# A hybrid decoder layer in fp32r on one core: delta-rule rows turned by VectorE and stored by token, early cache loads, a new first load order and regrouped gate products

## The reference

```
proj = x @ w_in          # A q/k/v | B q/k/v | B z | beta | a | gates
A: dilated attention, 3 groups x 4 heads x 64; samples attend to cached keys and values
B: gated DeltaNet, 4 heads of 128: causal conv (4 taps) + SiLU on q/k/v,
   k, q divided by their norm; beta = sigmoid, decay = exp(-exp(A_log) softplus(a + dt))
   kk = (k beta) k^T ; L = strict_lower(kk * decay) + I ; u = solve(L, v beta - ...)
   attn = (q k^T) * decay ; S = S g + k_dec^T u ; o = q_dec S + attn u
   o = rmsnorm(o) * w * silu(z)
merged = gate_a * (o_att @ w_att_out) + gate_b * (o_dn @ w_dn_out)
h = LN1(alpha x + merged @ w_o)
y = LN2(alpha h + (gelu(conv3(h W_a) + b) * (h W_g)) @ w_down)
```

## Time and profile before

| what | value |
|---|---|
| median of 3 runs | 1831.82 us (1828.69 to 1833.61) |
| the profiled execution | 1833.33 us, span 1831.5 us |
| TensorE (PE) busy | 1772.1 us, 97% of the span |
| VectorE (DVE) busy | 862.7 us, 47% |
| ScalarE (ACT) busy | 539.8 us, 29% |
| GpSimd (POOL) busy | 367.3 us, 20% |
| mean granted TensorE clock | 0.987 |
| moved by DMA | 169.17 MB, mean 92 GB/s |

### The profile page before, as it was taken

The page is one execution under the profiler, slowest core; times in us unless marked ns, Lnnn a source line. Parts: engine busy times, 40 slices in busy tenths (PEclk is TensorE's granted clock), DMA queues, the critical chain, the costliest instruction groups (busy, mean ns, idle before and its releaser), DMA issues.

```text
span 1831.5 us, 36738 instructions
## 1 busy us (share of the span) xinstructions
PE 1772.1 (97%) x14932; PEld 1716.6 (94%) x14932; DVE 862.7 (47%) x1573; ACT 539.8 (29%) x1086; POOL 367.3 (20%) x176
## 2 busy tenths in 40 slices
PE   7999999999988999999999999999999999999997
PEld 6999999999977888888999999999999999999996
DVE  2003347675264667765574674441144441144447
ACT  3124334444412333331222342221022221022224
POOL 1121111121111101011132342222222222222230
PEclk9999999999989999999999999999999999999998
DMA  4110112242442323224462113334332111111112
GB/s 175 46 46 30 44 55 79 81 171 98 138 149 86 112 75 112 76 69 169 143 230 81 70 52 122 123 125 145 122 121 97 46 46 47 46 47 46 38 45 93
DMA packets 70015, 169.17 MB, mean 92 GB/s; under 512 B 9440, under 2 KB 41344, under 8 KB 68608
## 3 DMA queue, kind: packets, MB, share of 16 engines
q1 hardware_dynamic: 69184, 166.63, 26.7%
q10 hardware_dynamic: 720, 0.93, 0.1%
HBM read 137.15 MB, written 57.79 MB: 106 GB/s over the span
## 4 chain that ended last, share of the span: by engine, by line
PE 88%; DVE 6%; DMA 2%; issue 2%; ACT 1%; POOL 1%; SPq 0%; DVEq 0%; ACTq 0%; POOLq 0%
PE U L764 57%; PE U L868 8%; PE U L1201 4%; PE U L1296 3%; PE B L764 2%; PE B L854 1%; PE B L829 1%; PE B L846 1%; PE B L1031 1%; PE B L1063 1%; DVE acc L2134 1%; ACT acc L1569 1%; PE B L1159 1%; DVE og L1825 1%; DVE X L1972 0%
## 5 line engine op out<-in xcount | busy, mean ns | idle before, releaser
L675 POOL TENSOR_TENSOR wl<-stage,wh 128x1024 fp32r<-128x1024 f32 x121 | 296.0, 2446 | 1051.9 <-ACT wh L1313 1049.2
L764 PE MATMUL U<-xh,wh 128*128 128x344 f32 x1176 | 383.1, 326 | 0.2 <-ACT qkv L1317 0.2
L764 PE MATMUL U<-xl,wh 128*128 128x344 f32 x1176 | 376.3, 320 | 0.0
L764 PE MATMUL U<-xh,wl 128*128 128x344 f32 x1176 | 376.2, 320 | 0.0
L764 PE MATMUL U<-hh,wh 128*128 128x344 f32 x1048 | 335.9, 321 | 0.3 <-POOL wl L675 0.3
L764 PE MATMUL U<-hh,wl 128*128 128x344 f32 x1048 | 334.5, 319 | 0.0
L764 PE MATMUL U<-hl,wh 128*128 128x344 f32 x1048 | 334.3, 319 | 0.0
L764 PEld LDWEIGHTS U<-xh,wh 128*128 128x128 f32 x1176 | 221.7, 188 | 0.7 <-ACT qkv L1317 0.5
L764 PEld LDWEIGHTS U<-xh,wl 128*128 128x128 f32 x1176 | 221.7, 189 | 0.0
L764 PEld LDWEIGHTS U<-xl,wh 128*128 128x128 f32 x1176 | 221.6, 188 | 0.0
L764 PEld LDWEIGHTS U<-hh,wh 128*128 128x128 f32 x1048 | 197.2, 188 | 0.8 <-issue 0.8
(11 more groups left out here) (381 smaller groups left out, 2754.5 us busy)
## 6 DMA issues: line engine op xcount, KB each, us to landing
stage<-in_wu SPq DMA_DIRECT2D x126, 512.0 KB, 3.6
out_shift<-in_cache SPq DMA_DIRECT2D x16, 1022.0 KB
gate_scr<-gth SPq DMA_DIRECT2D x16, 516.0 KB, 3.0
gates<-gate_scr SPq DMA_DIRECT2D x8, 1032.0 KB, 5.0
dn_scr<-thb SPq DMA_DIRECT2D x12, 512.0 KB, 2.6
qkv<-in_xT SPq DMA_DIRECT2D x4, 1032.0 KB, 10.5
out_y<-acc SPq DMA_DIRECT2D x12, 344.0 KB, 2.4
kvc<-in_cache SPq DMA_DIRECT2D x4, 1024.0 KB, 9.1
```

The costliest lines, as they stand in the source:

```text
L675: nc.gpsimd.tensor_tensor(wl[:, par, :], stage[:, par, :], wh[:, par, :].bitcast(F32), ALU.subtract).then_inc(w_lo, 1)
L764: ins = nc.tensor.matmul(dst, a[:, par, w], col, start=first and n == 0 and m == 0, stop=last and n == len(ks) - 1 and m == 2)
```

## The change

1. **Turn beside attention.** After `silu` of a q, k or v row block, VectorE turns `thb` in blocks of 32x32 into the `pre` buffer of the block before. SP stores it in four pieces to a new array `tok_scr` (12 row blocks, 1024 tokens by 128 features). ScalarE waits for these stores before it refills that buffer.
2. **Delta tiles.** `kq_turned` and `v_turned` load keys, queries and values by token. The twelve transposes of a tile go. ScalarE makes the squares from SBUF (`squares`), and also `kd` and `vp` (`key_sides`, `value_sides`), at levels 2 and 4. VectorE's key norms of the next tile stand at the end of a tile. The turned output goes to another bank (B7 in place of B34), and `late_masks` comes ahead of the first addition.
3. **Sample group.** The cached keys are loaded in blocks 20 and 21 into the part of `qkv` that is free then, the values at the start of the stage. The decay coefficients (`cf`, `gT`) and the first tile's decays are made inside this stage, not behind it.
4. **Gate quarters.** New counts: `S_FILLS` and `FILLS`.
5. **Start.** The first weights are loaded ahead of x, x in pieces of 1, 1, 2 and 4 tiles; the high products of the first unit come ahead of those of `wbr`.

The diff, cut to its core (memory places, declarations and the parts of the sample group that only rename its tiles are left out):

```diff
+        S_FILLS = (5, 3, 21, 27, 4)
...
-        FILLS = {1: (0, 2, 4, 1, (1, 1, 2, 1, 1, 2), 2), 2: (2, 4, 6, 2, (2, 1, 2, 1, 1, 3), 4)}
+        FILLS = {1: (0, 0, 4, 1, (2, 0, 2, 0, 0, 2), 2), 2: (0, 0, 8, 2, (2, 1, 2, 1, 1, 3), 4)}
...
-            for i in range(4):
-                sp.dma_start(xraw[:, 2 * i:2 * i + 2, :], I["xT"][:, 2 * i:2 * i + 2, :]).then_inc(x_in[i], 16)
-                if i == 0:
-                    sp.dma_start(stage[:, 0, :], I["wu"][0]).then_inc(w_in[0], 16)
+            sp.dma_start(stage[:, 0, :], I["wu"][0]).then_inc(w_in[0], 16)
+            for i, (a, b) in enumerate(X_PIECES):
+                sp.dma_start(xraw[:, a:b, :], I["xT"][:, a:b, :]).then_inc(x_in[i], 16)
...
+            def turned_out(f, par):
+
+                sp.wait_ge(rows_turned, f + 1)
+                for q in range(4):
+                    dst = tok_scr[bass.ds(f, 1)].squeeze(0).rearrange("(n t) (q e) -> q t n e", t=QB, e=QB)[q]
+                    sp.dma_start(dst, pre[QUARTER[q], par, 3:3 + SEQ].rearrange("t (n e) -> t n e", e=QB)).then_inc(
+                        turned_stored[par], 16)
...
+            def cached(n, dst, sems):
+
+                g, t = ((0, 0), (0, 1), (2, 0), (1, 0), (1, 1))[n]
+                a = dst is vals
+                src = I[f"cache{g}"].rearrange("b (c j d) e -> (b c) j d e", c=16, d=DIL[g][1])
+                sp.dma_start(dst[:, n], src[:, 4 * t:4 * t + 4, 0, 256 * a:256 * a + 256]).then_inc(sems, 16)
...
+                if isinstance(b, int) and b in (2 * BLOCKS + 4, 2 * BLOCKS + 5):
+                    sp.wait_ge(kv_stored, 48)
+                    for m in ((0, 1) if b == 2 * BLOCKS + 4 else (2, 3, 4)):
+                        cached(m, keys, samp_in)
...
+                    if kind == "dn" or first_z:
+                        turned_out(b - (BLOCKS + 1), 1 - par)
...
-            for x in range(EARLY - 1):
-                load(U_GATE + 3 + x, (x + 1) % 2)
-                gate_out(U_GATE + x, x % 2)
-            sp.wait_ge(samp_pe, 6)
-            sp.dma_start(dcst[:], I["dcst"]).then_inc(dcst_in, 16)
...
+            def kq_turned(t):
+                sp.dma_start(qkt[:], tok_scr[0:8, t * P:(t + 1) * P, :].rearrange("f t e -> t f e")).then_inc(kq_in, 16)
+
+            def v_turned(t):
+                sp.dma_start(dv[:], tok_scr[8:12, t * P:(t + 1) * P, :].rearrange("f t e -> t f e")).then_inc(v_in, 16)
...
+            load(U_GATE + 2, 0)
+            for n in range(SK // 4):
+                cached(n, vals, values_in)
+            kq_turned(0)
             qk_rows(0)
-            v_rows(0)
-            gate_out(U_GATE + EARLY - 1, (EARLY - 1) % 2)
+            v_turned(0)
             sp.wait_ge(g_turned, 1)
             sp.dma_start(g_scr.rearrange("t (h q) -> (t h) q", h=DN_H), gT[:]).then_inc(g_stored, 16)
             sp.wait_ge(g_stored, 16)
             decays(0)
+            for x in range(EARLY - 1):
+                load(U_GATE + 3 + x, (x + 1) % 2)
+                gate_out(U_GATE + x, x % 2)
+            gate_out(U_GATE + EARLY - 1, (EARLY - 1) % 2)
             for i, u, units in tiles():
                 load(u + 2, u % 2)
...
-                    sp.wait_ge(front_done, i * 4 + 2)
-                    v_rows(i + 1)
                     sp.wait_ge(decay_weighted, i + 1)
                     decays(i + 1)
                     after(sp, ks_done, i)
                     qk_rows(i + 1)
+                    sp.wait_ge(kd_ready, i + 1)
+                    kq_turned(i + 1)
                 for x in range(1, units):
                     gate_out(u + x - 1, (u + x - 1) % 2)
                     load(u + x + 2, (u + x) % 2)
+                if i + 1 < TILES:
+                    sp.wait_ge(vp_ready, i + 1)
+                    v_turned(i + 1)
                 gate_out(u + units - 1, (u + units - 1) % 2)
             sp.wait_ge(s_ready, TILES + 1)
...
-            pe.wait_ge(wba_split, 2)
             for k in range(KT):
                 w = slice(k * P, (k + 1) * P)
                 first, last = k == 0, k == KT - 1
                 pe.wait_ge(x_hi, k + 1)
                 for j in range(THIRDS):
+                    nc.tensor.matmul(U[:, j, 0:TW], wh[:, 0, w], xh[:, k, third(j)], start=first, stop=False)
+                if first:
+                    pe.wait_ge(wba_split, 2)
+                for j in range(THIRDS):
                     nc.tensor.matmul(ba_bank[j], wbr[:, k, :], xh[:, k, third(j)], start=first, stop=False)
-                for j in range(THIRDS):
-                    nc.tensor.matmul(U[:, j, 0:TW], wh[:, 0, w], xh[:, k, third(j)], start=first, stop=False)
...
-            beside.run(30)
+            beside.run(S_FILLS[1])
+            pe.wait_ge(dcst_in, 16)
+            gall = babuf[:, 1, 0:TILES, :]
+            tri = dcst[:, D_TRI:D_TRI + P]
+            nc.tensor.matmul(B7[:, 0:32], tri, gall, start=True, stop=True)
+            nc.tensor.matmul(B7[:, 32:64], dcst[:, D_ONE:D_ONE + P], gall, start=True, stop=True)
+            nc.tensor.matmul(B56[0:DN_H * TILES, 0, 0:P], gall.rearrange("p t h -> p (t h)"), tri, start=True,
+                             stop=True).then_inc(cf_pe, 1)
+            beside.run(S_FILLS[2])
+            pe.wait_ge(g_turned, 1)
             pe.wait_ge(samp_dve, 1)
...
-                    ins = nc.tensor.transpose(B34[:, 1, c], of[:, h, :], ident)
+                    ins = nc.tensor.transpose(B7[:, c], of[:, h, :], ident)
...
-                if i < TILES:
-                    pe.wait_ge(dn_in, 32 * i + 32)
-                    after(pe, xt_ready, i * (LEVELS + 1))
-                    for h, c in heads:
-                        ins = nc.tensor.transpose(B7[:, c], dqk[:, i % 2, 4 + h, :], ident)
-                    ins.then_inc(front_done, 1)
-                    beside.run(f_turn)
+                after(pe, xt_ready, i * (LEVELS + 1))
...
-                for h, c in heads:
-                    ins = nc.tensor.transpose(B56[:, 1, c], dv[:, h, :], ident)
-                ins.then_inc(front_done, 1)
-                for h, c in heads:
-                    ins = nc.tensor.transpose(B56[:, 0, c], dqk[:, i % 2, h, :], ident)
-                ins.then_inc(front_done, 1)
                 beside.run(f_keys)
-                after(pe, of_ready, i - 1)
+                pe.wait_ge(dn_in, 16 * i + 16)
+                after(pe, o_ready, i - 1)
                 pe.wait_ge(ao_low, i + 1)
...
+                        if kind == "dn" or isinstance(b, int) and b < 2 * BLOCKS + 6:
+                            after(act, turned_stored[par], (b - (BLOCKS + par)) * 32)
...
+            def squares(t):
+                act.wait_ge(kq_in, 16 * t + 16)
+                nc.scalar.activation(sqk[:], qkt[:, 4:8, :], ACT.Square, scale=0.5).then_inc(squared, 1)
+                nc.scalar.activation(qkt[:, 0:4, :], qkt[:, 0:4, :], ACT.Square, scale=0.5).then_inc(squared, 1)
...
+            def key_sides(t):
+                act.wait_ge(decay_weighted, t + 1)
+                for h in range(DN_H):
+                    ins = nc.scalar.activation(kd[:, t % 2, h, :], qkt[:, 4 + h, :], ACT.Identity, bias=0.0,
+                                               scale=rn[:, 11, h:h + 1])
+                ins.then_inc(kd_ready, 1)
+
+            def value_sides(t):
+                act.wait_ge(k_rooted, t + 1)
+                act.wait_ge(v_in, 16 * t + 16)
+                for h in range(DN_H):
+                    ins = nc.scalar.activation(vp[:, t % 2, h, :], dv[:, h, :], ACT.Identity, bias=0.0,
+                                               scale=rn[:, 2, h:h + 1])
+                ins.then_inc(vp_ready, 1)
...
+                    if lv == 2:
+                        key_sides(i)
                     if lv == 3 and i + 1 < TILES:
                         decay_of(i + 1)
+                    if lv == 4:
+                        value_sides(i)
...
+                if i + 1 < TILES:
+                    squares(i + 1)
...
+                    if kind == "dn" or first_z:
+                        dve.wait_ge(conv_out, b - (BLOCKS - 1))
+                        nc.vector.transpose(pre[:, 1 - par, 3:3 + SEQ], thb[:, 0:SEQ]).then_inc(rows_turned, 1)
...
+                if n == 0:
+                    dve.wait_ge(cf_act, 1)
+                    st.link(nc.vector.tensor_copy(cf[:, 0, 0:32], B7[:, 0:32]))
+                    nc.vector.tensor_tensor(cf[:, 3, 0:32], B7[:, 32:64], cf[:, 0, 0:32], ALU.subtract).then_inc(cf_dve, 1)
+                    nc.vector.tensor_scalar(cf[:, 4, 0:32], cf[:, 0, 0:32], -1.0, None, ALU.mult).then_inc(cf_dve, 1)
...
+            def decay_rows(t):
+                dve.wait_ge(g_in, 16 * t + 16)
+                nc.vector.tensor_tensor(ET[:], ET[:], same(dcst[:, D_NEG:D_NEG + P]), ALU.add).then_inc(decay_sum, 1)
+
+            decay_rows(0)
...
+                if t > 1:
+                    out_gated(t - 2)
...
-                dve.wait_ge(k_rooted, t + 1)
-                dve.wait_ge(front_done, t * 4 + 2)
```

(10 more changed lines are left out.)

201 lines of the change are left out of this document (87 added, 114 removed).

## The result

| | before | changed |
|---|---|---|
| median of 4 runs | 1832.27 us | 1816.26 us (1815.48 to 1817.69) |
| ratio, 95% interval | 1 | 0.9912 (0.9893 to 0.9932) |
| the profiled execution | 1833.33, span 1831.5 | 1815.48, span 1813.6 |

The account below looks back on a forecast made before the run. TensorE, busy 97% of the span, was taken as the bound. Gains of 2.4 + 7.0 + 7.3 + 9.8 + 4.6 = 31.1 us, from a median of 1831.8, gave 1801 us, range 1788 to 1816.

Parts of the forecast that it names:

- the weighted values end in time: Sample group: with 27 quarters TensorE's wait of 4.5 us for VectorE's weighted values falls to 1.6, and the clock stays.
- the decay row costs 0.4 us: Sample group: VectorE may wait for a decay row queued on SP behind values and rows; 0.4 us set against the gain.
- the first rival: Delta tiles: with the fills gone, levels wait on Y copies and X additions, 1.5 us a tile: 1813, chance 0.13.
- Start, forecast 2.4: Before TensorE's first product: loads ahead of the weights' copy fall from 1544 to 512 KB, gaining 2.4 us.
- Blocks, forecast 0: Twelve attention blocks: VectorE's turn of 1.32 us fits its wait, stores of 3.8 us a block hide behind it; cost 0.
- Sample group, forecast 7.0: Earlier cache loads, moved quarters, a shorter wait for the values and the full clock behind it gain 7.0 us.
- my rival: Sample group: slower strided reductions or a decay row 4 us late keep the wait and lower clock: 1808, chance 0.12.
- First tile, forecast 7.3: The mask wait of 4.7 us goes, with 1.3 of half clock and 1.3 for the twelve transposes.
- the third rival: TensorE's issue pauses of 3.7 us and the slow products round them vanish: 1795, chance 0.08.
- Tiles 1 to 7, forecast 14.4: Fewer transposes and less switching win 1.4 us a tile, 9.8 in all; the wait at the turned output another 4.6.
- I leave the issue pauses in: First tile's forecast: TensorE's issue pauses of 3.7 us are kept in the forecast time.
- The signs: Observations listed beforehand as showing the forecast right, such as first product near 7.4 and tiles 28 us apart.

Follow-up runs that it names:

- x_again: The changed kernel itself, unedited, run once more on the chip of the last group: 1815.37 us, ratio to before 0.9900.
- x_kv_early: Changed kernel, but SP stores keys and values of two of the three groups eight blocks earlier: 1809.90 us, ratio to before 0.9877.
- x_long_runs: Changed kernel, but turned rows are stored as they lie, in 4 KB runs, so the order by token is lost: 1815.57 us in one run.
- x_decay: Changed kernel, but VectorE adds the mask to the first tile's decay rows behind the sample's weighted values; it also waits for all five value loads: 1813.54 us, 0.9878.
- x_sample: Changed kernel with the edits of x_mask and x_decay, the sample's own value product ahead of the cached ones and 34 quarters instead of 27: 1804.09 us, 0.9832.
- x_mask: Changed kernel, but in each tile ScalarE copies the next unit's weights before the gated output, not after it: 1805.84 us, ratio to before 0.9857.
- x_loads2: x_mask, but SP makes all three loads of the next tile at the end of a tile: 1816.38 us, ratio to before 0.9908.
- x_all_loads: x_sample with the early store of x_kv_early, zero products before the first, and the load by features at a tile's end: 1800.05 us, 0.9817.

## Why the prediction was wrong, step by step

The steps that failed are two: in the sample group, that the weighted values end in time and the decay row costs 0.4 us, and in the tiles, that VectorE's product for the mask keeps its length when the order changes. The levels were not left bare, as the first rival had it: TensorE's waits there for the addition to X are 3.1 us in 16 places, and were 4.5 in 23. That the median lies so near the range's end, and that of x_again (1815.37) inside it, is luck: no case of the prediction had this mechanism.

**Start, forecast 2.4, measured 1.6.** The first product came 2.19 us earlier (9.83 to 7.64), as worked from the 1032 KB less. What the sum took for granted is that all products behind it move with it. Their slow pace of 0.287 us lasted 1.1 us longer in this execution, which at half speed is the 0.55 that is missing. In x_again it was shorter, and the start won 2.9. So 2.4 was a fair size.

**Blocks, forecast 0, measured -1.7.** The turn was sized well: 1.25 us against 1.32, and it delayed nothing. The Trainium skill (VectorE: DVE Perf Modes, The three transpose paths) led to an estimate of 2.5 us, twice what the f32 turn of 128x1024 takes. At that price the turn would be 1.0 us late in half of the blocks by the prediction's own counting, which makes 6 us and not the 4 it gives. The runs of 128 bytes cost 8 ns, not 15, the price at which I called them hidden. The stores took 4.0 us to landing in the median, but up to 8.6, not within 6. What failed is "they hide behind a block": I compared a block's mean load with its length, and 3.4 MB of outputs leave within one block's time. Undisturbed blocks are still 13.68 apart; blocks 16 and 17 are not, and the 1.5 us there go when either stream is eased (x_kv_early, x_long_runs).

**Sample group, forecast 7.0, measured 0.1.** From the samples' turn to the end of the products for their output it is 59.33 us, and 61.09 before. But 16 gate products (2.5 us) more lay in the old stage, while the coefficients (0.8) are in the new one: nothing is won in this execution, and some 4 more where the products are not held. Two terms were mis-sized. The decay row, "0.4", cost 2.6 us of TensorE's wait and 1.6 more at the lower clock behind it: I had seen the queue of values and rows ahead of it on SP, but not that VectorE's whole softmax stands behind the row (x_decay). And "the weighted values end in time" failed by the two held products, 1.9 and 1.6 us. The reductions over two strided axes, on which my rival rested, were nearly as before: 4.11 against 3.83. With both mended the group gives 8.9 (x_sample), more than the 7.0. So the rival's effect came, in part by the cause that it named second and in part by one that it did not name.

**First tile, forecast 7.3, measured 10.7.** The wait of 4.7 and its clock went as worked. Of the 3.4 beyond the forecast, 3.0 are the pause of 1.30 at 583 and 1.7 us by which products behind it were slow in the kernel before. I had left them in, and they did not come back in this tile. That is luck: the third rival had it so.

**Tiles 1 to 7, forecast 14.4, measured 4.5.** An undisturbed tile won 1.13, where 1.4 and the 0.66 of L945 were worked; without the wait of 1.09 at the mask it is 2.26 (x_mask), so the transposes, the fills and the turned output were priced rightly in sum. The step that failed is not in the text: with the fill between the turned output and the keys gone, GpSimd's subtraction starts 2.64 us behind the first key product and not 1.22 (696.76 against 695.54 in tile 4 of the kernel before), so 1.75 us of it are left when L1937 starts, and not 0.3. I had never placed it on the clock. In tile 1, where no gated output holds up ScalarE's copy, the wait is 0.15, and the profile of before already had L1891 at 1.16 in tile 0. 6.7 us went there. Another 3.5 went to pauses: tiles 2 to 7 lost 5.8 us beyond their undisturbed length, 2.3 before. "I leave the issue pauses in" took them for a constant. Most pauses over 0.8 us end where an instruction packet comes behind a burst of loads, and the change put 512 KB more into the levels; that the loads cause them is likely from x_loads2 and x_all_loads, not shown. x_again lost 3.19 in one pause and 7.2 in all. Its six runs span 9.8 us, of which pauses and the order in the sample group may both be causes; only one run has a trace.

**Behind the tiles, forecast 0, measured 2.7.** 1.6 in the ninth step and 1.1 in the samples' delta step. In both the kernel before had a stretch of granted clock below 1.00 (0.82 and 0.75 from 814 to 822, 0.50 from 844 to 846) that the changed one has not. At the first a wait of 1.03 at 813.98 is gone: I had counted the wait and not its clock, and all profiles of the changed code have the gain. Of the rest nothing can be said, since the same code varies by 6.6 us there.

**The signs.** Right were the first product near 7.4, the turn of 1.3, no wait at the first tile's mask or at the turned output. Wrong were no wait on ScalarE, all stores landing within 6 us, a wait under 2 at the values with the full clock behind it (0.50 from 540 to 542), and tiles 28 apart.
